# Router logits from raw rows, and the rows for DRAM made inside expert 0, in a two-layer transformer trunk

## What is computed

```python
x_lat = x_lat + ms[2] * rmsnorm(o_lat, post_mix_g[l])
f_lat = rmsnorm(x_lat, pre_ffn_g[l]) * (1 + ms[4]) + ms[3]      # modulate
logits = f_lat @ router_w
top_v, top_i = lax.top_k(logits, 2)
top_w = softmax(top_v)
y = sum over the experts e: gate[:, e] * ((silu(f_lat @ w1[e]) * (f_lat @ w3[e])) @ w2[e])
x_lat = x_lat + ms[5] * rmsnorm(y, post_ffn_g[l])
```

## Time and profile before

| | |
|---|---|
| runs | 1740.7, 1742.97, 1743.19 us; median 1742.97 |
| profiled execution | 1742.21 us, its span 1740.4 us |
| busy: TensorE, VectorE, ScalarE, GpSimd | 1702.7, 1406.1, 1094.9, 78.1 us |
| granted TensorE clock, mean | 0.996 |
| DMA | 504.73 MB, 290 GB/s in the mean |

### The profile page before, as it was taken

How to read it: one execution, slowest core, us unless ns; L and a number is a source line. 1 busy time by engine, 2 the same in 40 slices (tenths; PEclk the granted TensorE clock), 3 DMA queues, 4 the chain that set the end, 5 groups by cost and what they waited for, 6 DMA issues and landing times.

```text
span 1740.4 us, 24303 instructions
## 1 busy us (share of the span) xinstructions
PE 1702.7 (98%) x8034; PEld 1380.6 (79%) x8034; DVE 1406.1 (81%) x1655; ACT 1094.9 (63%) x1401; POOL 78.1 (4%) x92
## 2 busy tenths in 40 slices
PE   7999999999999999999999999999999999999997
PEld 4876878888788877778888888888888888888885
DVE  4947677385664589769999999999999999999998
ACT  4435552222222354658888888888888888888886
POOL 0114000000010000310000000000000000000001
PEclk9999999999999999999999999999999999999999
DMA  9858736364574447269999999999999999999995
GB/s 346 281 162 303 265 95 197 105 182 132 157 230 155 126 125 266 75 231 373 383 361 395 385 368 394 376 376 391 366 390 383 362 396 384 369 393 372 381 379 189
DMA packets 229200, 504.73 MB, mean 290 GB/s; under 512 B 16192, under 2 KB 47040, under 8 KB 228848
## 3 DMA queue, kind: packets, MB, share of 16 engines
q1 hardware_dynamic: 225152, 492.78, 79.2%
q0 software_dynamic: 3968, 10.94, 2.1%
HBM read 496.81 MB, written 19.95 MB: 297 GB/s over the span
## 4 chain that ended last, share of the span: by engine, by line
PE 93%; DVE 4%; ACT 1%; issue 1%; DMA 1%; SPq 1%; DVEq 0%; ACTq 0%
PE ps L638 29%; PE ps L640 28%; PE ps L639 28%; PE ps L1161 1%; PE ps L899 1%; PE ps L934 1%; DVE w_lo L1657 1%; DMA raw<-in_ada_w 1%; PE ps L922 0%; PE ps L665 0%; PE ps L658 0%; PE ps L1130 0%; PE ps L685 0%; PE ps L1103 0%; PE ps L882 0%
## 5 line engine op out<-in xcount | busy, mean ns | idle before, releaser
L1657 DVE TENSOR_TENSOR w_lo<-raw,w_hi 128x1024 fp32r<-128x1024 f32 x570 | 685.2, 1224 | 168.4 <-ACT w_hi L1239 141.1
L1560 ACT ACTIVATE w_hi<-raw 128x1024 fp32r<-128x1024 f32 x448 | 473.1, 1061 | 100.3 <-PE ps L640 100.2
L638 PE MATMUL ps<-w_hi,he_hi 128*128 128x512 f32 x896 | 353.7, 395 | 0.8 <-DVE w_lo L1657 0.8
L640 PE MATMUL ps<-w_hi,he_lo 128*128 128x512 f32 x896 | 349.5, 390 | 0.0
L639 PE MATMUL ps<-w_lo,he_hi 128*128 128x512 f32 x896 | 348.8, 389 | 0.0
L1657 DVE TENSOR_TENSOR w_lo<-raw_more,w_hi 128x1024 fp32r<-128x1024 f32 x224 | 273.6, 1225 | 31.1 <-ACT w_hi L1560 12.2
L1560 ACT ACTIVATE w_hi<-raw_more 128x1024 fp32r<-128x1024 f32 x224 | 237.8, 1062 | 50.8 <-PE ps L640 50.8
L1239 ACT ACTIVATE w_hi<-raw 128x1024 fp32r<-128x1024 f32 x122 | 128.4, 1059 | 195.7 <-PE ps L640 182.6
L640 PEld LDWEIGHTS ps<-w_hi,he_lo 128*128 128x128 f32 x896 | 168.2, 188 | 35.9
L638 PEld LDWEIGHTS ps<-w_hi,he_hi 128*128 128x128 f32 x896 | 168.2, 188 | 34.5 <-DVE w_lo L1657 1.2
L639 PEld LDWEIGHTS ps<-w_lo,he_hi 128*128 128x128 f32 x896 | 168.4, 188 | 33.8
(11 more groups left out here) (276 smaller groups left out, 1962.9 us busy)
## 6 DMA issues: line engine op xcount, KB each, us to landing
raw<-in_moe_w SPq DMA_DIRECT2D x448, 512.0 KB, 6.0
raw_more<-in_moe_w SPq DMA_DIRECT2D x224, 512.0 KB, 5.9
raw<-in_ada_w SPq DMA_DIRECT2D x96, 512.0 KB, 4.4
raw<-in_ffn_w SPq DMA_DIRECT2D x66, 512.0 KB, 4.5
raw<-in_w_in SPq DMA_DIRECT2D x40, 512.0 KB, 5.6
raw<-in_w_out SPq DMA_DIRECT2D x16, 512.0 KB, 6.6
yrows<-in_x SPq DMA_DIRECT2D x9, 512.0 KB, 16.3
xe<-xrows SPq DMA_DIRECT2D x7, 512.0 KB, 6.5
```

The source lines that it names most:

```text
L638: pe.matmul(o, lh, rh, start=start, stop=False)
L640: return pe.matmul(o, ll, rh, start=False, stop=stop)
L1560: act.activation(w_hi[:, s % SPL, :], expert_raw(i), ACT.Copy).then_inc(hi_done, 1)
L1657: dve.tensor_tensor(w_lo[:, s_ % SPL, :], src, w_hi[:, s_ % SPL, :].bitcast(F32), ALU.subtract)\
```

## The change

The logits are made from the raw residual rows: (x * r) * a + b times W equals r * (x times aW) + bW. VectorE scales router_w by the modulation (`rw_a`) and sums the shift's part (`rw_b`) before the last attention step (`scale_router`), which needs router_w loaded earlier by GpSimd. TensorE turns `xs` itself (`turn_x`), VectorE and ScalarE copy a half each (`xT`), and the logits come with tokens on partitions, with the 8 columns of `rw_a` repeated 16 times as the moving operand. Expert 0's tokens are gathered from the unmodulated rows `xn` and modulated after the gather, pair by pair of 128-column tiles, by ScalarE (`split_first`); VectorE's splits of units 1 to 3 stand between the low parts. The modulated rows for the scatter are made by VectorE in steps 1 to 4 of expert 0 (`modulated_rows`), from rows of the modulation that GpSimd stores to DRAM and loads back to all partitions; they are read with a step of 8 words. `destinations` moves from the end of `route` to before `token_gates`. SyncE takes expert 1's rows at unit 72 instead of 40. Roots take sums of squares: scale 1/D, and as bias eps or the other half's mean plus eps (`rest`), so that the add and mean on VectorE go (`pre_mean`, `post_mean`, `head_mean`, L2248, L2249; at the end one of two steps). `turn_h` with its filler, `modulate_h`, the modulation at L2280 and ScalarE's copies to `hrow` go; 6 and 3 filler products are put around the ranks.

```diff
-        rw = place("rw", [P, KD, 32], F32, Z + 36864)
-        hrow = place("hrow", [P, NLAT, D], F32, Z)
+        rw = place("rw", [P, KD, NE], F32, CST + 4 * C_COS)
+        rw_a = place("rw_a", [P, KD, NE], F32, CST + 4 * (C_COS + 64))
+        rw_b = place("rw_b", [P, NE], F32, CST + 4 * (C_COS + 128))
+        shifted = place("shifted", [P, NE], F32, CST + 4 * (C_COS + 136))
+        hrow = place("hrow", [P, NLAT, D], F32, Z + 16384)
+        xT = place("xT", [P, NLAT, KD, P], F32, Z + 24576)
+        mod_rows = place("mod_rows", [P, 2, D], F32, X + 8192)
...
+                        if i == (XIN_FIRST if first and not turn else XIN_AT) and not last:
...
+            link(pool.tensor_copy(mod_cols[:, 0, :], mod_a[:, 1, 1, :, 0]))
+            link(pool.tensor_copy(mod_cols[:, 1, :], mod_b[:, 1, 1, :, 0]))
+            for i in range(2):
+                pool.dma_start(mrows[i].rearrange("(p k) -> p k", p=P), mod_cols[:, i, :]).then_inc(sg("mod rows"), 16)
+            pool.wait_ge(sg("rope"), 4 * NLAT)
+            pool.wait_ge(sg("mod rows"), 32)
+            pool.dma_start(rw[:, :, :], router_w[0].rearrange("(k p) e -> p k e", p=P)).then_inc(sg("mod rows"), 16)
             spatial_norms(1)
             gate_rows(2)
-            pool.wait_ge(unit_used, NS0)
-            link(pool.memset(rw[:, :, :], 0.0))
-            pool.dma_start(rw[:, :, 0:NE], router_w[0].rearrange("(k p) e -> p k e", p=P)).then_inc(sg("ws in"), 16)
+            pool.wait_ge(sg("scores"), len(items[0]) + len(items[1]))
+            pool.wait_ge(sg("mod rows"), 48)
+            for i in range(2):
+                pool.dma_start(mod_rows[:, i, :], mrows[i].partition_broadcast(P)).then_inc(sg("mod rows"), 16)
             pool.wait_ge(sg("rows filled"), 32 * NE + 16)
-            pool.wait_ge(sg("hrow"), NLAT)
+            pool.wait_ge(sg("hrow"), 2 * NLAT)
...
+            def turn_x(tb, half):
+
+                bank = (4, 0)[tb] + half
+                for k in range(4 * half, 4 * half + 4):
+                    m = pe.transpose(ps[:, bank, P * (k % 4):P * (k % 4) + P], xs[:, tb, P * k:P * k + P], ident)
+                m.then_inc(sg("xT ps"), 1)
+
+            def logits(tb, ks):
+
+                for k in ks:
+                    if k == 0:
+                        pe.wait_ge(sg("xT dve"), tb + 1)
+                    if k == 4:
+                        pe.wait_ge(sg("xT act"), tb + 1)
+                    m = pe.matmul(ps[:, (6, 3)[tb], 0:P], xT[:, tb, k, :], rw_a[:, k, :].unsqueeze(1).to_broadcast([P, P // NE, NE]),
+                                  start=(k == 0), stop=(k == KD - 1))
+                if ks[-1] == KD - 1:
+                    m.then_inc(sg("logits"), 1)
...
+                pe.wait_ge(sg("rw scaled"), 1)
+                pe.matmul(ps[:, 7, 0:NE], ones, rw_b[:, :], start=True, stop=True).then_inc(sg("logits"), 1)
+                pe.wait_ge(sg("x mix1"), 2)
+                turn_x(0, 0)
+                turn_x(0, 1)
+                logits(0, range(0, 6))
+                pe.wait_ge(sg("x mix1"), 3)
+                turn_x(1, 0)
+                pe.wait_ge(sg("x mix1"), 4)
+                turn_x(1, 1)
+                logits(0, range(6, KD))
+                logits(1, range(0, 4))
+                logits(1, range(4, KD))
+                pe.wait_ge(sg("z pm1"), 2 * NLAT)
                 pe.matmul(ps[:, 2, P:2 * P], ones_r[:, :], triu_r[:, :], start=True, stop=True)
+                keep_warm(6, ps[:, 7, 0:P])
                 pe.wait_ge(sg("mask"), 1)
                 pe.matmul(ps[:, 2, 8:16], ones_r[:, :], mask_r[:, 0:8], start=True, stop=False)
...
-                pe.wait_ge(sg("hrow"), NLAT)
+                pe.wait_ge(sg("xn ffn1"), NLAT)
                 pe.wait_ge(sg("perm"), NLAT)
                 for k in range(KD):
                     for tb in range(NLAT):
-                        m = pe.matmul(ps[:, 4 + k // 4, P * (k % 4):P * (k % 4) + P], hrow[:, tb, P * k:P * k + P], perm[:, tb, :],
+                        m = pe.matmul(ps[:, 4 + k // 2, P * (k % 2):P * (k % 2) + P], xn[:, tb, P * k:P * k + P], perm[:, tb, :],
                                       start=(tb == 0), stop=(tb == NLAT - 1))
-                    if k % 4 == 3:
+                    if k % 2:
                         m.then_inc(sg("gathered"), 1)
...
-                act.wait_ge(sg("ms " + key), b + 1)
-                act.activation(st[:, 8 + b:9 + b], st[:, 4 + b:5 + b], ACT.Sqrt).then_inc(sg("rt " + key), 1)
+                act.wait_ge(sg("ss " + key), b + 1)
+                act.activation(st[:, 8 + b:9 + b], st[:, b:b + 1], ACT.Sqrt, scale=1.0 / D, bias=eps).then_inc(sg("rt " + key), 1)
...
+            def norm_before_experts():
+
+                for tb in range(NLAT):
+                    if tb:
+                        act.wait_ge(unit_used, last_s(("out", 1, 1)) + 1)
+                    else:
+                        act.wait_ge(sg("out"), NB)
+                    act.wait_ge(sg("ss pm1"), NLAT + tb)
+                    act.activation(ptmp[:, 0:512], ps[:, 2 * tb + 1, :], ACT.Square, accum_out=st[:, 20 + tb:21 + tb])\
+                        .then_inc(sg("ss pm1"), 1)
+                    act.wait_ge(sg("ss pm1"), NLAT + tb + 1)
+                    act.wait_ge(sg("rest pm1"), 1)
+                    act.activation(st[:, 24 + tb:25 + tb], st[:, 20 + tb:21 + tb], ACT.Sqrt, scale=1.0 / D, bias=st[:, 32 + tb:33 + tb])\
+                        .then_inc(sg("rt pm1"), 1)
+                    if tb:
+                        keep_xT(0)
+                        split_expert_unit(0, 0, 0)
+                    for half in range(2):
+                        o = slice(512 * half, 512 * half + 512)
+                        act.wait_ge(sg("x mix1"), 2 * tb + half + 1)
+                        act.activation(xn[:, tb, o], xs[:, tb, o], ACT.Square, accum_out=st[:, 4 * half + tb:4 * half + tb + 1])\
+                            .then_inc(sg("ss ffn1"), 1)
+                    if tb:
+                        keep_xT(1)
+                    act.wait_ge(sg("ss ffn1"), 2 * tb + 2)
+                    act.wait_ge(sg("rest ffn1"), tb + 1)
+                    act.activation(st[:, 8 + tb:9 + tb], st[:, 4 + tb:5 + tb], ACT.Sqrt, scale=1.0 / D, bias=st[:, 57 + tb:58 + tb])\
+                        .then_inc(sg("rt ffn1"), 1)
+                act.wait_ge(sg("last rstd"), 1)
+                act.activation(xn[:, 1, :], xs[:, 1, :], ACT.Identity, scale=st[:, 13:14]).then_inc(sg("xn ffn1"), 1)
+
+            def split_first():
+
+                for pair in range(KD // 2):
+                    act.wait_ge(sg("gathered"), pair + 1)
+                    for k in (2 * pair, 2 * pair + 1):
+                        act.activation(he32[:, k, :], ps[:, 4 + pair, P * (k % 2):P * (k % 2) + P], ACT.Identity,
+                                       bias=mod_b[:, 1, 1, k, 0:1], scale=mod_a[:, 1, 1, k, 0:1]).then_inc(sg("he32"), 1)
+                    act.wait_ge(sg("he32"), 2 * pair + 2)
+                    act.activation(he_hi[:, 2 * pair:2 * pair + 2, :], he32[:, 2 * pair:2 * pair + 2, :], ACT.Copy).then_inc(sg("he hi"), 1)
...
+            def rest(key, n):
+
+                dve.wait_ge(sg("ss " + key), n)
+                dve.tensor_scalar(st[:, 32:32 + n], st[:, 16:16 + n], 1.0 / D, EPS, ALU.mult, ALU.add).then_inc(sg("rest " + key), 1)
...
+                dve.tensor_tensor(rw_a[:, :, :], rw[:, :, :], mod_a[:, 1, 1, :, 0:1].to_broadcast([P, KD, NE]), ALU.mult)
...
+            def norm_before_experts():
+
+                rest("pm1", NLAT)
+                for tb in range(NLAT):
+                    if tb:
+                        dve.wait_ge(sg("logits"), 1)
+                        dve.tensor_copy(shifted[:, :], ps[:, 7, 0:NE])
+                        dve.wait_ge(sg("xT ps"), 1)
+                        dve.tensor_copy(xT[:, 0, 0:4, :], ps[:, 4, :].rearrange("p (k t) -> p k t", t=P)).then_inc(sg("xT dve"), 1)
+                    dve.wait_ge(sg("ss pm1"), NLAT + tb + 1)
+                    dve.tensor_tensor(zmix[:, tb, 512:1024], ps[:, 2 * tb + 1, :], gg[:, gate_at(1, 0, 0), 512:1024], ALU.mult)\
+                        .then_inc(sg("z pm1"), 1)
+                    dve.wait_ge(sg("rt pm1"), tb + 1)
+                    link(dve.reciprocal(st[:, 28 + tb:29 + tb], st[:, 24 + tb:25 + tb]))
+                    dve.wait_ge(sg("z pm1"), NLAT + tb + 1)
+                    for half in range(2):
+                        o = slice(512 * half, 512 * half + 512)
+                        dve.scalar_tensor_tensor(out=xs[:, tb, o], in0=zmix[:, tb, o], scalar=st[:, 28 + tb:29 + tb], in1=xs[:, tb, o],
+                                                 op0=ALU.mult, op1=ALU.add).then_inc(sg("x mix1"), 1)
+                    dve.wait_ge(sg("ss ffn1"), 2 * tb + 1)
+                    dve.tensor_scalar(st[:, 57 + tb:58 + tb], st[:, tb:tb + 1], 1.0 / D, EPS, ALU.mult, ALU.add).then_inc(sg("rest ffn1"), 1)
+                    if tb:
```

(45 more changed lines are left out.)

199 lines of the change are left out of this document (73 added, 126 removed).

## The result

The changed kernel takes 1744.85 us (median of 22 executions), the kernel before 1741.62 beside it: ratio 1.0018, 95% interval 1.0012 to 1.0024. One of the 22 of each kernel took over 2800 us (the changed kernel's at a granted clock of 0.557) and is left out of the ratio. It was forecast 8 us faster and is 3 us slower. The execution followed here took 1745.38 us, its span 1743.6.

A forecast was written before the change was run, and what follows sets the result against it. TensorE's rate bounds the experts; the router stretch before them can shrink. Gains 6.0 + 1.35 + 0.26 + 0.3 + 0.4 less 0.2 make 8.1 us; 1742.2 less 8.1, plus 0.76, gives 1734.9 us, range 1732.3 to 1740.3.

The forecast's parts named there:

- What bounds the kernel: Experts run at TensorE's rate; the 20.5 us between output projection and expert 0, plus the fifth unit's wait, are reachable.
- the router: Between output projection and expert 0's fifth unit: expert 0 starts 6.8 us earlier, 6.0 remain, bounds 5.0 to 6.8.
- gather at full clock: Gather of expert 0's tokens: 32 passes in 3.6 us at full clock, instead of 5.44 at half clock.
- The smaller terms: Outside the router: shorter root chains gain 1.35, 0.26, 0.3 and 0.4 us; the row modulations cost 0.2.
- Dense FFN: After the dense FFN: the root follows the square and TensorE's wait goes; gain 1.35 us, bounds 0.6 to 1.9.
- head: Head norm in layer 1: TensorE's wait for the head's rows goes; gain 0.3 us, bounds 0 to 0.35.
- mixer: After layer 0's mixer: the chain behind TensorE's wait gets shorter; gain 0.26 us, bounds 0 to 0.4.
- the tail: At the kernel's end: the link between add and mean falls in both blocks; gain 0.4 us, bounds 0.3 to 0.45.
- The modulated rows: Steps 1 to 4 of expert 0: modulations take 1.2 us each and fit the cover; 0.2 us lost in all.
- The rival: Row modulations in expert 0: strided SBUF reads at half rate, 2.2 us each, 4.3 in all, 1739.0 us; chance 0.25.
- The scatter: Expert 0's scatter: done at 865.5, SyncE waits 4.8 us, 0 charged; rival that it comes late and slows, chance 0.05.
- The clock: Router: half clock in the gather or pairs at 1.3 us leave a gain of 5.0, 1736.8 us; chance 0.12.

The follow-up runs named there:

- e4: The kernel before with 55 matrix products added in a branch that is never executed: 1746.74 us.
- e7: The changed kernel with VectorE products at several steps from SBUF and PSUM, and scatter issues, measured after its last add; no kernel time given.
- e3: The changed kernel with twelve matrix products added in the branch that is not executed: 1739.78 us, ratio to before 0.9989.
- e1: The changed kernel with the modulation's rows stored in column order, so read with a step of one word: 1741.32 us, ratio to before 0.9997.
- e6: The changed kernel with rows in column order and eight filler products before expert 0's fifth unit: 1735.05 us, ratio to before 0.9967.
- e5: The changed kernel itself, run again beside the others: 1744.54 us, ratio to before 1.0017.
- e2: The changed kernel with eight filler products in the wait before expert 0's fifth unit: 1739.77 us, ratio to before 0.9988.
- e9: The changed kernel with seven chains of VectorE instructions after its last add, GpSimd's scatter issued during the third instruction of each; no kernel time given.
- e10: e6 with the four row modulations moved from steps 1 to 4 to steps 2 to 5 of expert 0: 1744.82 us.
- e11: The changed kernel with five further VectorE chains after its last add, GpSimd's issue released by the chain's own product; no kernel time given.

## Why the prediction was wrong

**What bounds the kernel, and the router: right.** First product of expert 0 6.93 us earlier (forecast 6.8), 5.74 left at the fifth unit (6.0), gather at full clock, pairs 1.15, wait 1.95: each within 0.3. Part of the gather's gain is luck, since the half clock that it is counted against comes in some executions of the kernel before only (e4 had none).

**The smaller terms: right in sum.** Dense FFN 1.16 for 1.35, head 0.50 for 0.3, mixer 0.22 for 0.26, and the tail without its gap 13.5 to 13.8 us against 14.0 to 14.1: 0.2 to 0.6 for 0.4. Together about 2.3 for 2.3. VectorE's timeline after the FFN shows it: 1.41 us from gate product to residual in the earlier trace rows, 0.80 now:

```profile
609.84 0.69 DVE L1895 TENSOR_TENSOR y<-y,gg 128x512 f32<-128x512 f32 x1 [0.86 <-ACT sgf L1337]
...
610.64 1.28 DVE L1974 SCALAR_TENSOR_TENSOR xs<-y,st,xs 128x1024 f32<-128x1024 f32 x1
```

**The modulated rows: the failed step.** "A modulation is a 1024-wide product of two SBUF operands like the split" left out the step of 8 words. The only strided row I had was a reduction in PSUM, and I let it speak for SBUF, though I wrote beside it that it was PSUM. e7 shows both halves: PSUM reads at 1.22 us at every step, SBUF needs 2.0. The rival priced it rightly (2.2 us each, 1.07 beyond the cover, 4.3 in all; measured 2.15, 1.13, 4.5), and its time, 1739.0, is near that of e3, 1739.78, which has no gap; as a gain on the kernel beside it, it is 4.0 for a measured 1.8. Nor was "I take 0.2 in all" right for contiguous rows: e1 and e6 lose 0.2 a step, 0.8 in all, so of the 4.5 some 3.8 are the step of 8 words. The rival had a chance of 0.25 on a row from the wrong memory. The Trainium skill's page "SBUF — State Buffer" (section "Door 1: The DMA port swizzle") pointed the right way, and the trace agrees with its direction; the limit, by e7, is lower than the four words it gives: 2 is free, 4 isn't.

**The place of the code: missing from the sum.** Nothing in my working looked at what a shorter instruction list does. TensorE executes 8016 products for 8034 before, its code moved, and in the last rows a gap of 2.2 to 2.9 us opened. That an edge of a block of instructions came to lie there is the likely reason and isn't shown; that the place makes the gap is. In the medians e5 is 4.8 us above e3, with the clock that falls behind the gap and whatever else differs between their executions. The trace of before had the fetches of instructions in its DMA queues; I read these only for the scatter. Either failure alone is enough to undo most of the forecast. With the strided rows alone (e3) the change gives 1739.78, 0.11% faster; with the gap alone (e1) 1741.32, no difference; with both it is slower. Without the gap the time would have lain inside the range.

**The scatter: right in kind, two sizes off.** Its waits were 1.05 us in the followed execution, 0.64 in e2, 0.22 in e5 and 0 in e3, since it ended at about the point where it begins to count. I had it done at 865.5 on the old clock; it was 872.1 (871.6 in the trace). The 7.5 us issue explains a part only: with an issue of 1.8 the scatter still took 15.3 us from its first issue in e1 and e9 and 16.1 in e6, and ended at 869.6 to 870.5 on the old clock, where I took 11.8 us from the trace of before. SyncE reached the take where I said, at 860.3 on the old clock for 860.7, and waited 11.8 us (e1: 9.4) for a forecast of 4.8. What kept this cheap is that the point lay 2.5 to 4.4 us later than my 868.5 (e10).

**The clock: forecast in the wrong place.** I looked for it in the gather, where it stayed full; it fell after the fifth unit's wait, which I had sized at 1.8 and charged nothing for. It cost 1.6 us where it came, in four of the seven traces with that wait.

## What to carry over

Before you cost a vector instruction like its neighbour, compare the access patterns as well as shape and memory: with fp32 in SBUF a step of 4 words or more cost a product 54 to 64% (e7), and storing the small operand in the other order once removes it. A row from PSUM is no evidence for SBUF. When a change is judged by a few microseconds, look for a gap that ends in "issue", and put some never-executed instructions ahead of it: if the time moves, part of what you have measured is the place of the code and not the change.

## What was not expected of the hardware

- A gap of 2.2 to 2.9 us between two TensorE products, made and unmade by code that never runs (e3, e4). Without it the medians are 4.8 us lower, the clock that falls behind it included.
- SBUF against PSUM at a step: 1.97 and 1.22 us for 1024 elements at a step of 4.
- Scalar products of one SBUF operand with a step of 8, in a row, kept GpSimd's issue out for 9.47 us; contiguous ones for 1.15.
- The same wait of 1.9 us was followed by half clock in the changed kernel, e5, e7 and e9, and not in e1, e3 and e11. The gather of the kernel before ran at half clock in two traces and at full clock in e4.
- The first scatter issue took 7.46 us in five traces with strided rows and 1.78 in two others with the same rows.
